# The query projection of the matrix memory, moved to later fill places and made in three rounded passes

## The reference, cut to what matters

```python
xc = heads(jax.nn.silu(causal_conv(m_x, ml_conv_w)), ML_HEADS)
q = jnp.einsum('blhd,hde->blhe', xc, ml_wq.astype(f32))
k = jnp.einsum('blhd,hde->blhe', xc, ml_wk.astype(f32))
...
    k = k * dh ** -0.5
    s = jnp.einsum('bhrd,bhsd->bhrs', qc, kc) * w
```

## Time and profile before

| | |
|---|---|
| time, median of 3 runs | 1772.15 us (1770.97 to 1772.45) |
| time of the profiled execution | 1769.98 us |
| its span, first to last instruction | 1767.8 us |
| TensorE busy | 1728.8 us (98%) |
| VectorE, ScalarE, GpSimd busy | 1034.6, 594.2, 538.2 us |
| mean granted clock of TensorE | 0.998 |

### The profile page before, as it was taken

The page is one execution under the profiler, slowest core; times in us unless marked ns, Lnnn a source line. Parts: engine busy times, 40 slices in busy tenths (PEclk is TensorE's granted clock), DMA queues, the critical chain, the costliest instruction groups (busy, mean ns, idle before and its releaser), DMA issues.

```text
span 1767.8 us, 22844 instructions
## 1 busy us (share of the span) xinstructions
PE 1728.8 (98%) x8848; PEld 1438.5 (81%) x8848; DVE 1034.6 (59%) x2022; ACT 594.2 (34%) x829; POOL 538.2 (30%) x342
## 2 busy tenths in 40 slices
PE   6989999999999999999999999999999999999998
PEld 5878888888787888888888788888878878888886
DVE  7889726562383477339847886253723825862625
ACT  5332334451125113432144332544311341143320
POOL 2543403022121313345355432121212141224451
PEclk9999999999999999999999999999999999999999
DMA  7435363242023206774433433541411222268441
GB/s 276 138 107 150 95 217 136 91 120 84 25 89 126 96 25 226 227 267 162 143 127 125 134 113 103 214 179 38 131 48 48 96 104 87 70 225 288 167 169 57
DMA packets 98707, 235.23 MB, mean 133 GB/s; under 512 B 10912, under 2 KB 41968, under 8 KB 97064
## 3 DMA queue, kind: packets, MB, share of 16 engines
q1 hardware_dynamic: 71688, 182.15, 30.5%
q10 hardware_dynamic: 26832, 51.39, 8.0%
q0 software_dynamic: 80, 0.23, 0.0%
HBM read 170.55 MB, written 58.98 MB: 130 GB/s over the span
## 4 chain that ended last, share of the span: by engine, by line
PE 85%; DVE 7%; DMA 3%; ACT 2%; issue 1%; POOL 1%; SPq 0%; ACTq 0%; DVEq 0%
PE gp L627 21%; PE gp L629 20%; PE gp L628 20%; PE mm L629 2%; PE mm L628 2%; PE mm L627 2%; DMA wraw<-in_w 2%; PE mm L855 2%; PE mm L833 2%; POOL wlo L1144 1%; PE mm L879 1%; PE mm L782 1%; DMA yraw<-yt 1%; PE mm L783 1%; PE mm L784 1%
## 5 line engine op out<-in xcount | busy, mean ns | idle before, releaser
L1144 POOL TENSOR_TENSOR wlo<-wraw,whi 128x256 fp32r<-128x256 f32 (+1 forms) x270 | 444.5, 1671 | 1026.2 <-ACT whi L1222 1026.0
L627 PE MATMUL gp<-xh,whi 128*128 128x512 f32 x768 | 319.0, 415 | 1.1 <-ACT xh L1292 1.1
L629 PE MATMUL gp<-xh,wlo 128*128 128x512 f32 x768 | 301.1, 392 | 0.0
L628 PE MATMUL gp<-xl,whi 128*128 128x512 f32 x768 | 299.8, 390 | 0.0
L627 PE MATMUL gp<-whi,xh 128*128 128x512 f32 x640 | 269.1, 420 | 0.0
L1222 ACT ACTIVATE whi<-wraw 128x1024 fp32r<-128x1024 f32 x164 | 168.4, 1054 | 263.5 <-DMA wraw<-in_w 108.6
L629 PE MATMUL gp<-whi,xl 128*128 128x512 f32 x640 | 250.5, 391 | 0.0
L628 PE MATMUL gp<-wlo,xh 128*128 128x512 f32 x640 | 249.9, 391 | 0.0
L629 PEld LDWEIGHTS gp<-xh,wlo 128*128 128x128 f32 x768 | 144.2, 188 | 32.0
L627 PEld LDWEIGHTS gp<-xh,whi 128*128 128x128 f32 x768 | 144.9, 189 | 29.7 <-issue 3.1
L628 PEld LDWEIGHTS gp<-xl,whi 128*128 128x128 f32 x768 | 144.9, 189 | 25.7
(11 more groups left out here) (335 smaller groups left out, 2928.4 us busy)
## 6 DMA issues: line engine op xcount, KB each, us to landing
wraw<-in_w SPq DMA_DIRECT2D x164, 512.0 KB, 4.1
spill<-gate ACTq DMA_DIRECT2D x32, 512.0 KB, 2.9
yraw<-yt SPq DMA_DIRECT2D x32, 512.0 KB, 5.8
xs<-xr SPq DMA_DIRECT2D x16, 512.0 KB, 5.4
xraw<-in_xT SPq DMA_DIRECT2D x4, 1024.0 KB, 16.0
ud<-gate ACTq DMA_DIRECT2D x8, 512.0 KB, 2.6
uu<-ud SPq DMA_DIRECT2D x64, 64.0 KB, 2.6
p_tab<-kd SPq DMA_DIRECT2D x64, 64.0 KB
```

Of the source, the lines that this page charges most:

```text
L627: nc.tensor.matmul(out, ah, bh, start=start, stop=False)
L628: nc.tensor.matmul(out, ah, bl, start=False, stop=False)
L629: return nc.tensor.matmul(out, al, bh, start=False, stop=stop)
L1144: last = nc.gpsimd.tensor_tensor(wlo[slot(u)][:, w0 + c:w0 + c + n], raw_view(l, u, i)[:, c:c + n], whi[slot(u)][:, w0 + c:w0 + c + n].bit ...
```

## The change

It does five things.

- **Split of the product matrices.** ScalarE writes the scaled product as a rounded high part `wah` where `wqk` was; VectorE, before the convolution, writes the remainder `wal` out of the same PSUM bank.
- **Split of the channels.** For each head ScalarE rounds the SiLU's result into `xch` (`m_high`), and GpSimd subtracts it from `xc` into `xcl` (`conv_lo`); both have two buffers.
- **Three passes.** A projection is an `mm3` on the split parts in place of one float32 matmul.
- **Places.** The projections go from hooks 2 to 15 to hooks 8, 9, 12, 13, 16, 17, 20 and 21. On ScalarE the SiLU and rounding of heads 0 and 1 and the SiLU of head 2 stand before the weight split, the rounding of head 2 at hook 9, head 3's SiLU and rounding at hook 13. In GpSimd's order the four `conv_lo` stand among the remainders of U_LZ+1: head 0, weight half 0, head 1, weight half 1, head 2, head 3.
- **A merged semaphore.** The load of `mkT` counts on `aq_in0` in place of `mk_in`.

```diff
-        wqk = at("wqk", 1024, o_ys)
+        wqk, wah, wal = at("wqk", 1024, o_ys), at("wah", 512, o_ys, F32R), at("wal", 512, o_ys + 512, F32R)
+        xch = [at(f"xch{i}", T, R[2] + T * i, F32R) for i in range(2)]
+        xcl = [at(f"xcl{i}", T, R[2] + 2 * T + T * i, F32R) for i in range(2)]
...
-                sp.dma_start(mkT, dram["kvs"][:, 0:1024]).then_inc(S["mk_in"], 16)
+                sp.dma_start(mkT, dram["kvs"][:, 0:1024]).then_inc(aq_in[0], 16)
...
-                        pe.wait_ge(S["xc_ready"], 4 * l + h + 1)
+                        pe.wait_ge(S["xc_lo"], 4 * l + h + 1)
...
-                    nc.tensor.matmul(bank[2 + half], wqk[:, 128 * h:128 * h + 128], conv_view(h)[:, 4 * half:4 * half + 4, :],
-                                     start=True, stop=True).then_inc(S["qk_mm"], 1)
+                    a0, x0 = 128 * h, 512 * half
+                    mm3(bank[2 + half], wah[:, a0:a0 + 128], wal[:, a0:a0 + 128], xch[h % 2][:, x0:x0 + 512], xcl[h % 2][:, x0:x0 + 512],
+                        True, True).then_inc(S["qk_mm"], 1)
...
-                    if hook < 16 and hook % 4 in (2, 3):
-                        m_project(hook // 4, hook % 4 - 2)
+                    if 8 <= hook < 24 and hook % 4 < 2:
+                        m_project(hook // 4 - 2, hook % 4)
...
+            def conv_lo(l, h):
+
+                pool.wait_ge(S["xc_ready"], 8 * l + 2 * h + 2)
+                x = xch[h % 2].rearrange("p (c t) -> p c t", c=NC).bitcast(F32)
+                nc.gpsimd.tensor_tensor(xcl[h % 2].rearrange("p (c t) -> p c t", c=NC), conv_view(h), x, ALU.subtract).then_inc(S["xc_lo"], 1)
...
-                for u in range(U_RZ + 1, U_LO):
+                for u in range(U_RZ + 1, U_LZ + 1):
                     lo(l, u)
+                conv_lo(l, 0)
+                lo(l, U_LZ + 1, (0,))
+                conv_lo(l, 1)
+                lo(l, U_LZ + 1, (1,))
+                conv_lo(l, 2)
+                conv_lo(l, 3)
...
+                def m_high(h):
+                    act.wait_ge(S["xc_ready"], 8 * l + 2 * h + 1)
+                    if h >= 2:
+                        act.wait_ge(S["qk_mm"], 8 * l + 2 * h - 2)
+                    F(xch[h % 2].rearrange("p (c t) -> p c t", c=NC), conv_view(h), ACT.Copy).then_inc(S["xc_ready"], 1)
...
-                for h in range(3):
-                    m_silu(h)
+                m_silu(0)
+                m_high(0)
+                m_silu(1)
+                m_high(1)
+                m_silu(2)
...
+                dve.wait_ge(S["wa_ev"], 2 * l + 1)
+                STT(wal, bank[2], 128 ** -0.5, wah.bitcast(F32), ALU.mult, ALU.subtract).then_inc(S["wa_ev"], 1)
```

More of the change, by code:

```diff
@@ L266, in build @@
             sp_out0 sp_out1 gate_in0 gate_in1 gate_used0 gate_used1 rt_done rt_free yt_out0 yt_out1 yt_out2 yt_out3
-            mt_done mt_free mk_in mv_in aq_in0 aq_in1 xo_out xo_in ring_in ring_used
+            mt_done mt_free mv_in aq_in0 aq_in1 xo_out xo_in ring_in ring_used
             x_s x_max x_e x_norm x_t x_pt x_pv x_pvev xa_out wif_in
-            wif_hi wif_lo if_done if_act if_sum rows_done rf_out ab_in wa_ev res_in colt_done cols_done wqk_in conv_done xc_ready
+            wif_hi wif_lo if_done if_act if_sum rows_done rf_out ab_in wa_ev res_in colt_done cols_done wqk_in conv_done xc_ready xc_lo
             ones_done w_arg w_exp w_mask qk_mm qk_ev s_mm s_w k_tr k_w m_num m_read m_c m_st m_h gn_in uu_in0 uu_in1 yc_in0 yc_in1 yc_in2 yc_in3
@@ L827, in x_scores @@
                     if j % 8 == 0:
-                        pe.wait_ge(aq_in[j // 8], 32 * l + 32)
+                        pe.wait_ge(aq_in[j // 8], (48, 32)[j // 8] * (l + 1))
                     if j >= 2:
@@ L990, in m_project @@
                     if half == 0:
-                        pe.wait_ge(S["xc_ready"], 4 * l + h + 1)
+                        pe.wait_ge(S["xc_lo"], 4 * l + h + 1)
                     if h == 0 and half == 0:
-                        pe.wait_ge(S["wa_ev"], l + 1)
+                        pe.wait_ge(S["wa_ev"], 2 * l + 2)
                     if 2 * h + half >= 2:
                         pe.wait_ge(S["qk_ev"], n - 1)
-                    nc.tensor.matmul(bank[2 + half], wqk[:, 128 * h:128 * h + 128], conv_view(h)[:, 4 * half:4 * half + 4, :],
-                                     start=True, stop=True).then_inc(S["qk_mm"], 1)
+                    a0, x0 = 128 * h, 512 * half
+                    mm3(bank[2 + half], wah[:, a0:a0 + 128], wal[:, a0:a0 + 128], xch[h % 2][:, x0:x0 + 512], xcl[h % 2][:, x0:x0 + 512],
+                        True, True).then_inc(S["qk_mm"], 1)
                 def m_scores(c):
@@ L1544, in _ @@
                 act.wait_ge(S["colt_done"], 3 * l + 3)
-                F(wqk[:, 0:512], bank[2], ACT.Copy, scale=128 ** -0.5).then_inc(S["wa_ev"], 1)
+                F(wah, bank[2], ACT.Copy, scale=128 ** -0.5).then_inc(S["wa_ev"], 1)
                 x_evict(U_MX, 1)
@@ L1572, in weigh @@
                 def weigh(hook):
[L1574 to L1577, removed]
+                    if 8 <= hook < 24 and hook % 4 < 2:
+                        m_project(hook // 4 - 2, hook % 4)
+                    if hook in (9, 13):
+                        if hook == 13:
+                            m_silu(3)
+                        m_high(hook // 4)
                     if 17 <= hook < 25:
```

1 line of the change is left out of this document (removed).

## The result

The changed kernel took 1776.57 us (median of 8 runs, 1773.54 to 1778.7) beside 1770.8 us for the kernel before (8 runs, 1769.28 to 1773.83). The ratio is 1.003, with a 95% interval of [1.0019, 1.0041]: 3.4 to 7.3 us slower. The profiled execution took 1776.38 us, with a span of 1774.4 and a mean granted clock of 0.996.

A forecast was written before the change was run, and what follows sets the result against it. TensorE, busy 98% of the span, was taken as the bound. Per layer, stalls of 3.95 us less gains of 1.9 give +2.05, twice +4.1; on 1772.15 that is 1776.25, rounded to 1776.3 us, whole range 1771.5 to 1780.3.

The forecast's parts named there:

- second stall: TensorE in U_LZ, after the first projection: waits for weight half 1, 2.6 us, 2.7 with the restart, in each layer.
- head 1's remainder in the queue: GpSimd in U_LZ: head 1's channel remainder runs ahead of weight half 1; 2.4 of the 3.95 us of stalls.
- the later split against the earlier request: U_LZ: ScalarE splits weights 2.2 us later while TensorE asks sooner; the rest of the 3.95 us beside 2.4.
- Together 1.9 us: TensorE's gain per layer: 1.3 us from cheaper projections plus 0.64 us from the wait at hook 2.
- the wait at hook 2: TensorE's wait for head 0's SiLU disappears: 0.53 + 0.11 = 0.64 us gained per layer.
- eight times 0.16: Eight projections per layer, each three rounded matmuls at 0.69 us for 0.85: 1.3 us gained.
- a fourth pass: Bound on the rounded projection's price: 0.85 us with a fourth pass, no gain, 1.3 us less.
- What was said to cost nothing: VectorE's `wal`, 0.69 us, later roundings, evictions, exponentials, masks and queues were claimed covered, adding no time.
- The stall is smaller than summed: Rival: links on ScalarE, GpSimd or the passes slightly better; sum between 0 and +3.5, about 1774.5 us; chance 0.22.
- The remainders are in time: Rival: head 1's remainder and half 1 finish before TensorE's request; gain alone remains, -3.8 us, 1768.3; chance 0.07.
- The clock falls: Rival: TensorE's clock drops to the lower level behind the stalls, +1.25 us per layer, 1778.8 us; chance 0.11.
- The price of 1.25: Clock-fall cost per layer: a 2.5 us stretch at half clock does the work of 1.25, so +1.25 us.

The follow-up runs named there:

- e8: The changed kernel run again with nothing altered; one run, 1778.01 us.
- e2: Changed kernel with ScalarE splitting U_LZ+1's weights before head 0's SiLU, GpSimd's order left as changed; ratio 1.0028 to the kernel before.
- e7: Changed kernel with the channel remainders of heads 0 and 1 ahead of both weight halves on GpSimd; ratio 1.0038 to the kernel before.
- e1: Changed kernel with both weight halves of U_LZ+1 ahead of head 1's channel remainder on GpSimd; ratio 0.999 to the kernel before.
- e3: Changed kernel with ScalarE splitting the weights before the SiLUs and GpSimd making both weight halves before all heads; ratio 0.9986 to the kernel before.
- e5: e3 with every projection one place later (hooks 9, 10, 13, 14, 17, 18, 21, 22); ratio 0.9965 to the kernel before.
- e4: Kernel before with only the projections' new places, one plain float32 matmul each and no splits; ratio 0.9987 to the kernel before.
- e6: e2 with GpSimd's order half 0, head 0, half 1, head 1, then heads 2 and 3; ratio 0.9973 to the kernel before.

## Why the prediction was right or wrong

**The time** of 1776.57 us lies 0.3 from the forecast, and that closeness is luck. The forecast was +4.1 us on a base of 1772.15; measured are +5.8 us on a base of 1770.8, the median of more runs. And the difference is not made up as the forecast had it. Waits less gains are worth 2 x 1.66 = 3.3 us, where I had 4.1. The rest is the clock, a rival with a chance of 0.11, whose mark, a granted clock below 1.00 behind the second stall, I had named as a sign of being wrong. In the four profiles of kernels whose waits in U_LZ come to 2.8 us or more (changed, e8, e2, e7) it fell in 7 of 8 layers. The three falls of the changed kernel cost 1.60, 1.61 and 1.40 us against its layer without one: 2 x 7/8 x 1.54 = 2.7 us. Together 6.0, where the measurement says 5.8, interval 3.4 to 7.3. The interval takes in the 4.1 as well: it is the stretches that show what the time is made of, not the ratio.

**The waits** were right. TensorE asked for half 0 at 549.56 + 0.23 = 549.79 and went on at 551.01: 1.22 us, and 0.11 for the restart (551.01 to 551.35 for a pitch of 0.23); forecast 1.25 in all. On the time axis of the kernel before, 1.69 us earlier, these are 548.10 and 549.32, where the forecast had 548.2 and 549.35. It asked for half 1 at 553.19 and went on at 555.66: 2.47 + 0.11; forecast 2.7. The sum is 3.91 for 3.95. That head 1's remainder in the queue carries the larger wait is shown by e1. The smaller one I put down to "the later split against the earlier request". e2 shows that as too simple: with the split early the wait stays, since head 0's remainder is ahead of the weights. Only both moves together take it away (e3).

**The gain** was mis-sized. "Together 1.9 us" is 2.30 in e5 (42.21 - 39.91). The part of the wait at hook 2 was right (0.64, e4: 0.65). The step that was off is "eight times 0.16": it is 0.206. Of that 0.17 is the projection itself, 0.68 for 0.85 us. The remaining 0.036 is not in the projection's own row. In the kernel before, the five steps from 543.03, just behind a plain matmul, to 544.19 take 0.232 us each, and in the changed stream they take 0.227 (561.01 to 563.28, ten steps). Some seven such steps behind each projection make up the difference; that is argued from these rows and was not tried by itself. I had priced the plain matmul up to the start of the second matmul behind it and no further. One bound of this term was wrong too: a fourth pass at the stream's pitch would have been 4 x 0.229 = 0.92 us, not 0.85. No sum hangs on it.

**What was said to cost nothing** cost nothing: `wal` took 0.69 us before the convolution, the fourth head still waited for mx (3.25 us in place of 3.95), and no wait appeared at hooks 12, 16 or 20 or at the scores. VectorE's exponential arguments were stretched from 6.36 to 10.77 us, hidden. The other direction matters more. Head 0's remainder took 3.47 us beside a tap; the forecast had allowed for that and it cost nothing, as GpSimd then still waited 0.47 us for the weights. In e3 and e6 the same contention, with two to three taps, is what is left of the waits. For e3 my expectation had not allowed for it; for e6 it had, with a wait of up to 0.3 us for the 0.34 measured.

**The rivals.** "The stall is smaller than summed" holds for the net (3.3 for 4.1), by the gain and not by the stall. "The remainders are in time" came out nowhere in the changed kernel, and e5 shows what it would have been worth: 4.6 us, not 3.8. "The clock falls" was the one I gave too little, in chance and in price. I had two waits to compare with, 3.44 us with a fall and 1.90 without, and put the 2.6 between them; the later profiles have falls behind most waits from 2.00 us up. The price of 1.25 was half of the 2.5 us shown in the earlier trace rows, while the fall lasts 3.4 us in layer 0 of the changed kernel, at a pitch of 0.43 for 0.23.

## What to carry to other kernels

When small matmuls are moved out of the front half of a unit, the matmuls behind them ask for their weights earlier; so what prepares the weights has to be checked against the new time of the request, queue by queue. An instruction that is put into an in-order queue is paid for by everything behind it: put it in the order in which the consumer asks, and see whether its own input is ready, since waiting at the head of the queue costs like work. A wait of more than 2 us should be priced with a fall of the clock, which may come in one run and not in the next; here it cost 1.6 us, as much as the net loss of a layer without it.

## What the runs showed of the hardware

- TensorE's clock: single waits in U_LZ of 1.08 us (e1), 0.88 (e3) or 0.34 (e6) left it at full speed. Behind a wait of 1.06 or 1.37 us, 2 us of matmuls and a wait of 2.30 to 2.33 us it fell to the lower level for up to 3.4 us in five of six layers, the exception being layer 1 of the changed kernel's first profile; around one of 2.87 us it fell in two of two. Elsewhere it fell behind five of six waits of 2.00 to 2.55 us; two of these stand at the same place, 2.12 us with a fall (e5) and 2.13 without (e6).
- GpSimd and VectorE slow each other both ways. A channel remainder of 2.39 us took 3.47 beside a tap, two weight remainders 6.69 for 4.75, and two taps 4.63 for 2.61. In the earlier trace rows only VectorE had paid; its instructions there were short ones, 2.14 / 8 = 0.27 us each, which would fit but was not tried. This bears out the exclusive lock of the Trainium skill, "SBUF — State Buffer", section "SBUF: two separate sides", by which the later one waits for the whole instruction of the other: the 3.47 has 1.1 us more, close to what was left of a tap of 1.28 us that had started 0.09 us earlier. The ends of the taps and remainders in e3 fit such turns too.
- A projection as a plain float32 matmul costs the stream 0.89 us, by the stretches of e4 and e5 (0.68 + 0.206), where its own pitch is 0.85; that the rest falls on the matmuls behind it is argued above.
